# Pick work starts sixteen row sums later, and one 2 KB block moves from the mem_w_kv loads to the second-key loads

## The reference, cut to what matters

```
q = (xn @ wq).reshape(B, L, PH, PEER_DK)                 # 256 tokens, 8 heads
s1, s2 = q[first half] . k1, q[second half] . k2         # 128 keys each
...                                                      # top 16 pairs of a token and head
idx = i1 * 128 + i2                                      # which of 16384 experts
h = gelu(einsum('thkd,td->thk', U[idx], xn))             # one dot product per pick
w = gate * h
y = einsum('thk,thkd->td', w, V[idx])

kv = einsum("bmd,de->bme", mem_n, w_kv)                  # 256 x 2048 by 2048 x 2048
```

## Time and profile before

| | |
|---|---|
| time of the runs | 3690.56, 3692.9, 3693.02 us |
| profiled execution | 3695.03 us, its span 3693.3 us |
| PE busy | 3592.1 us (97%) |
| PEld busy | 3174.6 us (86%) |
| DVE busy | 2060.0 us (56%) |
| POOL busy | 967.2 us (26%) |
| ACT busy | 621.8 us (17%) |
| mean granted TensorE clock | 0.988 |
| first row sum of U / last | 1276.0 / 1992.4 us |

### The profile page before, as it was taken

How to read it: one execution, slowest core, us unless ns; L and a number is a source line. 1 busy time by engine, 2 the same in 40 slices (tenths; PEclk the granted TensorE clock), 3 DMA queues, 4 the chain that set the end, 5 groups by cost and what they waited for, 6 DMA issues and landing times. The chain is left out here.

```text
span 3693.3 us, 51125 instructions
## 1 busy us (share of the span) xinstructions
PE 3592.1 (97%) x20754; PEld 3174.6 (86%) x20754; DVE 2060.0 (56%) x4109; ACT 621.8 (17%) x1423; POOL 967.2 (26%) x813
## 2 busy tenths in 40 slices
PE   8999999999999999999888999999999999999999
PEld 6878877899998888888777777777799999999988
DVE  4883102055540399853698544444456766676653
ACT  0002102100002112221156200000222222222100
POOL 0000100101000156562887555455100022122000
PEclk9999999999999999999999999999999999999999
DMA  5434432344544699997897799999533422222352
GB/s 215 147 127 141 144 126 80 114 160 172 193 185 179 238 337 400 404 409 253 288 365 262 268 335 334 346 336 335 191 136 137 150 98 98 98 95 72 132 202 112
DMA packets 159014, 776.65 MB, mean 210 GB/s; under 512 B 19476, under 2 KB 21420, under 8 KB 122812
## 3 DMA queue, kind: packets, MB, share of 16 engines
q1 hardware_dynamic: 100536, 518.52, 38.5%
q0 software_dynamic: 57344, 251.69, 18.2%
q10 hardware_dynamic: 900, 3.17, 0.3%
HBM read 762.67 MB, written 10.64 MB: 209 GB/s over the span
## 5 line engine op out<-in xcount | busy, mean ns | idle before, releaser
L405 PE MATMUL PS<-mem,ring 128*128 128x272 f32 (+1 forms) x2816 | 649.6, 393 | 3.0 <-DMA ring<-in_first_tiles 3.0
L405 PEld LDWEIGHTS PS<-mem,ring 128*128 128x128 f32 x2816 | 543.1, 193 | 108.1 <-issue 5.3
L1281 POOL DMA_INDIRECT mem<-in_peer_ug,idx x256 | 346.7, 1354 | 537.1 <-DVE idx L1795 347.1
L1933 DVE SCALAR_TENSOR_TENSOR mem<-mem 128x768 f32<-128x768 f32 x256 | 261.0, 1020 | 285.6 <-DMA mem<-in_peer_vg,idx 279.7
L1848 DVE CUSTOM_DVE_ANT_0 mem<-mem 128x1152 f32<-128x1152 f32 x256 | 345.6, 1353 | 79.9 <-DMA mem<-in_peer_ug,idx 77.3
L1395 PE MATMUL PS<-mem 128*128 128x256 f32 x1792 | 387.2, 379 | 0.7 <-DMA mem<-in_peer_ud 0.7
L1395 PEld LDWEIGHTS PS<-mem 128*128 128x128 f32 x1792 | 340.3, 190 | 47.3 <-DMA mem<-in_peer_ud 1.1
L1307 POOL DMA_INDIRECT mem<-in_peer_vg,idx x256 | 281.5, 1100 | 277.3 <-DVE mem L1933 223.2
L413 PEld LDWEIGHTS PS<-mem,ring 128*128 128x128 f32 x3136 | 350.3, 192 | 0.1
L413 PE MATMUL PS<-mem,ring 128*128 128x128 f32 x3136 | 350.3, 275 | 0.0
L2279 PE MATMUL PS<-mem,ring 128*128 128x128 f32 x2560 | 312.3, 275 | 0.9 <-issue 0.6
(11 more groups left out here) (413 smaller groups left out, 4496.3 us busy)
## 6 DMA issues: line engine op xcount, KB each, us to landing
ring<-in_first_tiles SPq DMA_DIRECT2D x144, 1024.0 KB, 4.9
ring<-in_dn_tiles SPq DMA_DIRECT2D x88, 1024.0 KB, 5.0
mem<-in_peer_vd SPq DMA_DIRECT2D x128, 640.0 KB
mem<-in_peer_ud SPq DMA_DIRECT2D x128, 448.0 KB
ring<-in_out_panels SPq DMA_DIRECT2D x16, 2048.0 KB, 9.3
ring<-in_w_out SPq DMA_DIRECT2D x8, 2048.0 KB, 10.1
ring<-in_peer_wq SPq DMA_DIRECT2D x8, 2048.0 KB, 9.6
mem<-second_keys SPq DMA_DIRECT2D x64, 256.0 KB
```

What stands on the lines that cost most here:

```text
L405: last = nc.tensor.matmul(PS[:, 4 + n % 4, 0:T if wide else TX], wslots[slot_of[n]][:, k, :], x, start=(k == 0), stop=(k == KT - 1))
L1281: nc.gpsimd.indirect_dma_start(ugs[at % US], None, a["peer_ug"], bass.IndirectOffsetOnAxis(ap=idx[:, n, j:j + 1], axis=0)).then_inc(u_in[a ...
L1933: nc.vector.scalar_tensor_tensor(hc, Vg[:, at % GS, :], dots[:, m, h * PTOP + j:h * PTOP + j + 1], hc, ALU.mult, ALU.add).then_inc(vg_used, 1)
```

## The change

PICK0 goes from 11 * PTOP to 12 * PTOP (from step 176 to step 192). PG, the number of places for second keys, goes from 4 to 5. WK, the number of places for `mem_w_kv`, goes from 3 to 2. The new fifth place for second keys is the one that the third of `mem_w_kv` had, so the places are now a list. The pairs begin at step 202, not 186, and since they still end at step 253, 60 pairs now stand at 52 steps where they stood at 68.

```
-        CG, GU, KU, UT, BANKS_U, PG, PB = D - CD, D - CU, CU // P, 4, 4, 4, 3
+        CG, GU, KU, UT, BANKS_U, PG, PB = D - CD, D - CU, CU // P, 4, 4, 5, 3
...
-        oh = spot(27392, PG, 4, P)
+        ohs = [spot(27392 + 4 * P * s if s < 4 else MEM + 2 * GU, 4, P) for s in range(PG)]
...
-        NKV, KVB, MPS, WK = 8, (3, 5), KU // 2, 3
-        wkvs = [spot(29440 + 2 * PW * s if s < 2 else MEM + 2 * GU, 2, PW) for s in range(WK)]
+        NKV, KVB, MPS, WK = 8, (3, 5), KU // 2, 2
+        wkvs = [spot(29440 + 2 * PW * s, 2, PW) for s in range(WK)]
...
-        NPG, PICK0, PER, AHEAD = P // 4, 11 * PTOP, 4, 2
+        NPG, PICK0, PER, AHEAD = P // 4, 12 * PTOP, 4, 2
...
-                        sp.dma_start(oh[:, g % PG, :, :],
+                        sp.dma_start(ohs[g % PG],
...
-                                x = oh[:, g % PG, :, :].rearrange("p q k -> p (q k)")
+                                x = ohs[g % PG].rearrange("p q k -> p (q k)")
...
-                            last = nc.tensor.matmul(PS[:, g % PB, q * P:(q + 1) * P].rearrange("p (b l) -> p b l", l=LO), oh[:, g % PG, q, :],
+                            last = nc.tensor.matmul(PS[:, g % PB, q * P:(q + 1) * P].rearrange("p (b l) -> p b l", l=LO), ohs[g % PG][:, q, :],
```

## The result

| | before | after |
|---|---|---|
| median of 6 runs each | 3690.7 us (3684.2 to 3693.0) | 3701.3 us (3695.2 to 3709.6) |
| ratio, 95% interval | | 1.0031 [1.0018, 1.0044] |
| profiled execution, its span | 3695.0, 3693.3 us | 3695.9, 3694.2 us |

A forecast was written before the change was run, and what follows sets the result against it. PE, 97% busy, was taken as the bound, with 42 us of its idle time where the change acts. Terms 0 - 7 + 3 - 11 = -15 us gave 3678 us from a median of 3692.9; range 3662 to 3702.

The forecast's parts named there:

- Sixteen row sums into the gap (0): Gathers moved into POOL's 50 us wait before the first comparison cost nothing; bound one or two us if U tiles came late.
- Rival D: Moved gathers delay second keys and last U tiles, so pick work begins after 1728.7 us; chance 0.20 together with B.
- Early part (-7): First 128 tokens' 32 groups: a fifth place for second keys cuts POOL's and PE's waits; -7 us, bounds -13.6 and +12.
- Seam (+3): 1808 to 1827 us, around weight_transpose(0): two places start mem_w_kv loads one piece later; +3 us, bounds 0 and +5.4.
- Late part (-11): 1827 to 1993 us: DVE loses sixteen row sums, giving 155 us instead of 166; bounds -20.5 and +30.
- L: Latency of a mem_w_kv load in the late part, taken as 5.0 us between 3.7 and 9.6 seen in the trace.
- 22 x (L + 1.9) = 152: Late part's load limit with two places: 44 pieces, two per L + 1.9 us, 152 us beside DVE's 145.5 and PE's 142.
- PE's waits for `mem_w_kv` (15 to 25 us): Sign to check: in both later parts together these waits rise from 7.6 us to 15 to 25 us.
- V part: After the scatter, from 2054 us on: its first tile comes 15 us earlier and its length stays.
- A: Rival: two places are enough, with L at 4.3 us or less; -31 us, 3662 us; chance 0.20.
- B: Rival: two places are too few, L near 6.5 us; late part +19, in all +15, 3708 us; 0.20 with Rival D.
- C: Rival: no difference, as PE and DVE wait in turn for one-hot rows and loads; -3 us, 3690 us; chance 0.18.

The follow-up runs named there:

- e3: The changed kernel with a third place for mem_w_kv, in unused memory (start 192, five places for second keys): 3662.2 us, 0.9930 of the kernel before.
- e12: The changed kernel with three places for mem_w_kv, but the load for piece n+2 still starts only when piece n is done: 3697.1 us, 1.0025 of before.
- e1: The kernel before with only the start of the pick work moved (192; four places for second keys, three for mem_w_kv): 3670.7 us, 0.9946 of before.
- e5: The changed kernel with four places for second keys instead of five (start 192, two for mem_w_kv): 3704.8 us, 1.0046 of the kernel before.
- e14: e3 repeated on another chip: 3666.2 us, 0.9939 of the kernel before.
- e4: The kernel before with only a fifth place for second keys added (start 176, three places for mem_w_kv): 3687.0 us, 0.9986 of before.
- e8: The changed kernel with the pieces of mem_w_kv spread more evenly, some moved from the late into the early part: 3696.7 us, 1.0017 of before.
- e11: The changed kernel with each of its two mem_w_kv places loaded and released in halves of 128 KB: 3687.1 us, 0.9997 of the kernel before.
- e2: The kernel before with only the places changed (five for second keys, two for mem_w_kv; start still 176): 3714.3 us, 1.0063 of before.

## Why the prediction was wrong, by its own steps

**Sixteen row sums into the gap (0): right.** POOL's wait was 13.57 us (about 14 forecast, 50.2 before). In the U tiles PE waited once for `in_peer_ud`, 1.7 us, inside the bound of one or two, though a gap there had been named as a sign of being wrong. Rival D fell with it: the first comparison came 14 us after the gathers were out.

**Early part (-7): nearly right, -5.4.** POOL's other waits went from 18.8 to 25.9 - 13.6 = 12.3 us (under 8 forecast), PE's for comparisons from 13.6 to 5.3 (5 forecast). With three places for `mem_w_kv` it would have been -7.3 (e3, 76.0).

**Seam (+3): under-sized, +5.8.** That is just over the bound of 2 x 2.7 = 5.4. I had taken less because fewer loads would be queued; the load that decided still took 6.6 us, as the two of before had (6.7 and 8.6).

**Late part (-11): the step that failed, +1.4.** DVE's loss of row sums was right (145.5 forecast, 144.0 busy), and so was the latency, in part by luck, since no row gave a value between 3.7 and 9.6 for this part: I took L = 5.0, and the median from issue to landing of this part's loads is 4.9 us (DMA issues by destination, late part of after: how many, KB each, median us):

```profile
mem<-in_mem_w_kv SPq DMA_DIRECT2D x42, 256.0 KB, 4.9
```

What failed is what I did with L. "22 x (L + 1.9) = 152", set beside 145.5 and 142, with 3 added, treats the loads as a third engine that runs beside the others, so that the longest limit decides. But PE is in order and holds at most one loaded piece. Where it has a lot to do between piece n and n+2, the load is early and the surplus is lost; where it has 3.5 us, as at 1847, it stands for the rest. Without those waits PE has (168 - 22.2) / 44 = 3.3 us per piece, the piece itself included, so by this estimate 2 x 3.3 - 1.9 = 4.7 us between the end of piece n and the start of n+2: just L. With a mean slack of nothing, every piece whose cover was short of its load's time waited, 18 of 44 at 1.2 us each, and the others gave nothing back. These add to PE's own work: 138.3 + 22.2 + 7.4 = 168. That PE's 142 us of work and the load's limit lay so close should have been read as a sum with waits, and not as a maximum plus 3.

**PE's waits for `mem_w_kv` (15 to 25 us): 33.4.** This is the number that would have given the sum, had the forecast charged them to PE: 33.4 - 7.6 = 26 us more of waiting, where the forecast's -11 and +3 left room for hardly any.

**V part: right**, 607.1 against 606.2 us.

The Trainium skill, "DMA: Bandwidth & Descriptors", section "Anatomy of one DMA — SWDGE (gpsimd) path", would by the prediction's estimate have made two places ample: 2.6 us for 256 KB is below the 4.7 us that PE leaves. But that section gives its fit for DMAs issued by GpSimd, and these loads are issued by SP. The trace of after has, for its 64 loads of `mem_w_kv`:

```profile
DMA to landing us min/median/max: 2.7/4.8/8.4
```

The shortest are near 2.6 us; the median of the late part is 4.9 us at a DMA share of 0.83, and experiments e12 and e3 show that the start of the load against this latency is what costs.

**The rivals.** A (two places are enough, 3662 us) is refuted by after itself and e3: 3662 is what three places give. B had the right mechanism and sign (+19 in the late part at L = 6.5, 3708 us in all). Its condition, L above 5.8, was wrong: it happened at 4.9, for the reason above. What was to hold the equation back happened in part: the DMA share fell to 0.83. Whether L fell with it is not shown, as the trace of before has no landings to compare with. C's interplay of PE and DVE is not it: e3 has the same order and a late part of 147.0. I gave B with D 0.20; the four loads that I had followed (3.7, 6.7, 8.6 and 9.6 us) against a cover of some 5 us would have borne out at least as much as the forecast.

**The base.** The forecast stood on a median of 3692.9 us from three runs; with six it is 3690.7, so the same sum would give 3676, and the base hid 2 us of the miss.

**In the balance,** by the ratios, one edit at a time: the move gives 20 us (e1), the third place taken away costs 37 (e5), the fifth place gives 5.5 (after). In another order the fifth place gives 6 (e1 to e3; 3 by e14) and the third place costs 37 (e3 to after). The intervals of each pair that shows the fifth place overlap, so its gain is shown only by e4, -5 us, and barely. Not settled is why the pair of traces shows only 1.9 of these 11 us in the pick stage; with twelve runs of one kernel up to 23 us apart (e8), one pair of executions can't tell.

## What to carry to other kernels

Before you give up a place of a stream, compare the latency of its loads under this stage's load with the work that the consumer has between the release of a place and its next use, not with the average rate: here, where the two were equal on average, 18 of 44 loads were waited for, and more than half of the time was lost where the uses stood closest. Such waits on an engine that is nearly full add to its busy time; here the sum was right (168) and the longest of several limits was not (152 + 3). And when a change has several parts, run each alone: here -20 us was hidden behind +37, and the third place could be had from memory that lay unused.

## What the runs showed of the hardware beyond that

In the late part of e4 both the row sums and the comparisons took longer than in the kernel before, though their number was the same. Late part of e4 (busy us, mean ns), then that of before:

```profile
L1848 DVE CUSTOM_DVE_ANT_0 mem<-mem 128x1152 f32<-128x1152 f32 x69 | 100.9, 1469 | 3.4 <-ACT mem L1595 2.1 <-DMA mem<-in_peer_ug,idx 1.3
L1289 POOL TENSOR_SCALAR mem<-mem 128x512 f32<-128x512 f32 x28 | 66.3, 2366 | 0.9
```

```profile
L1848 DVE CUSTOM_DVE_ANT_0 mem<-mem 128x1152 f32<-128x1152 f32 x69 | 92.6, 1350 | 0.9 <-ACT mem L1595 0.9
L1289 POOL TENSOR_SCALAR mem<-mem 128x512 f32<-128x512 f32 x28 | 56.3, 2010 | 1.0
```

69 row sums at 119 ns more are 8.2 us. DVE's one-hot rows took 4.3 us less (47.0, not 51.3), so its busy time grew by 4.6 us, which is nearly the 5 us by which the part grew. The Trainium skill, "SBUF — State Buffer", section "Who interferes with whom", says that a DVE instruction with two inputs in SBUF contends with a GpSimd instruction that reads it. No run here took the overlap away, and nothing shows that the two overlapped more in e4 than before, so the cause stays open. In e11, with the loads in halves of 128 KB, the DMA share of the late part was 0.89, where after has 0.83. And the third place, measured three times, cost 37 us twice with the later start (e1 to e5, e3 to after) and 28 us with the early one (e4 to e2). The move gives 20 us with three places (before to e1, e4 to e3: 21) and 12 with two (e2 to after). So the parts add up within some 9 us, and with the intervals as wide as they are, that difference is not shown to be real.
